# Expert outputs weighted when they leave PSUM and added to rows of y by indirect DMAs

## Chip, cores and metric

One core of a Trainium2 chip (trn2). The metric is the device time of one execution in microseconds (us), as the median of several runs.

## What is computed

One inference step of a two-layer decoder on 288 tokens (256 of a prompt and 8 sequences of 4): an attention layer with a dense feed-forward layer, then a state space layer (S5) with a mixture of experts. The change is in the mixture of experts, the last stage:

```python
logits = xn @ w_router + b_router
top_v, top_i = lax.top_k(logits, 2)                      # 2 of 8 experts for each token
gates = softmax(top_v)
combine = sum(one_hot(top_i, 8) * gates[..., None], 1)   # weight of each expert for each token
out = zeros((288, 1024))
for e in range(8):
    h = silu(xn @ w_gate[e]) * (xn @ w_up[e])            # 1024 -> 2816
    out = out + combine[:, e:e+1] * (h @ w_down[e])      # 2816 -> 1024
y = hp + out                                             # hp: the residual
```

## The kernel before

The kernel is written by hand, engine by engine: each of the five engines has its own instruction list, and semaphores tie them. Weights come in float32 and are split into a high and a low part, so that a product takes three matmuls (high times high, low times high, high times low).

**The loop over experts.** An expert's tokens, at most 128 (`CAP`), fill slots 0 to 127. The 2816 hidden columns of an expert are 22 chunks (`NF`) of 128, and one loop of `ck` runs over the 8 x 22 chunks on every engine, with `n, j = divmod(ck, 22)`: expert `n`, chunk `j`. For each chunk SP loads 1536 KB of weights into one of 8 slots, as soon as the chunk 8 before it is done. ACT casts the high parts (`gate_up_high`, L1323, two chunks ahead; `down_high`, L1328), and DVE subtracts to get the low parts (`gate_up_low`, L1956, two chunks ahead; `down_low`, L1963). PE multiplies (`gate_up`, 24 matmuls, L948 to L950), transposes the hidden block of the chunk before (`turn`, L958) and multiplies it with the down weights of two chunks before (`down`, L967 to L969), which add up in two PSUM banks over the expert. ACT and DVE form the hidden block in between (L1334, L1971) and split its transpose (L1340, L1979).

**The next expert's tokens** are prepared inside the loop, at places set by three numbers, `J_SELECT, J_FIND, J_GATHER = 2, 4, 12`. At `j == 2` DVE makes a one-hot matrix of tokens against slots (`select_first`, L1882). At `j == 4` PE multiplies it with the token numbers and norm factors (`find`, L921), and DVE copies the result out (`index`, L1891 and L1892); POOL then fetches those rows of x with an indirect DMA (`gather`, L2119). At `j == 12` to `19` PE transposes one 128-column piece of the eight at the end of each iteration (`turn_row`, L937), ACT writes its high part (`gathered_one`, L1313) and DVE its low part (`gathered_one`, L1949, which signals `xg_lo`). At `j == 0` of the next expert PE waits for all eight low parts:

```python
for ck in range(NE * NF + 2):                  # tensor, L974
    n, j = divmod(ck, NF)
    if ck < NE * NF:
        if j == 0:
            pe.wait_ge(S["xg_lo"], (n + 1) * KD)
        gate_up(chunk_at(ck), n % 2)
```

On ACT and DVE `gathered_one` stands at the end of the iteration, behind `gate_up_high`, `down_high` and `gate_up_low`.

**The output.** In the second iteration of the next expert ACT copies the finished sums to SBUF (`expert_sum`, L1345) and stores them to a scratch tensor, `yrow` (L1347). On DVE, in the seventh iteration of the first expert, `weights_of` works out the gates and, for each token, the two scratch rows that hold its expert outputs and their weights (`ranks`), in a chain of small operations that each wait for the one before. At the end POOL fetches those rows in six indirect DMAs (`rows_of`, L2132), DVE multiplies and adds them to the residual `res` (`add_rows`, L1933), and SP stores y in three DMAs (L452). Rounds for experts with more than 128 tokens exist behind a branch on all engines, which this input does not take.

**Before the first expert** POOL's first gather waits for the rows of x to be in DRAM (`xrow`, stored by SP, L433 and L434) and for `index(0, 0)`.

Of the kernel before, what the change touches and what calls it, by code (L numbers as in the profile page):

```python
# [65 lines left out]
J_SELECT, J_FIND, J_GATHER = 2, 4, 12  # L66
# [11 lines left out]
def layout(parts):  # L78
    at, n = {}, 0
    for name, size in parts:  # L80
# [7 lines left out]
                        ("rsel", 2), ("tok", 3)])  # L88
# [87 lines left out]
def build(nc, dr):  # L176
# [22 lines left out]
    slots_of = nc.alloc_sbuf_tensor("slots_of", [P, 2, 6], I32)  # L199
# [71 lines left out]
    tr, rsl = v(M_RT + 224, 3, 2), v(M_RT + 232, 2)  # L271
    plg, ssq, gsel = v(M_RT + 400, 3, KD, 8), v(M_RT + 592, 3, KD), v(M_RT + 616, 2, 6)
# [44 lines left out]
    def past_values(b, j, p):  # L317
# [9 lines left out]
        wt xt_mm xnat xr route pos_mm rexp cnt mS find_mm mIdx xin mg_mm mgu msil mh my yout dest yin0 yin1 yin2  # L327
        radd out dve act""".split()
# [48 lines left out]
    def _(sp):  # L377
# [56 lines left out]
        sp.dma_start(dr["xrow"][TP:T, :], res[0:NS, 2, :]).then_inc(S["xr"], 16)  # L434
        for ck in range(MSLOTS, NE * NF):
            sp.wait_ge(S["unit"], U_PRE + ck - MSLOTS + 1)
            expert_load(ck % MSLOTS, ck)
        sp.wait_ge(S["cnt"], 1)
        more = sp.value_load(counts[0:1, 0:1], min_val=0, max_val=T)
        with sp.If(more > CAP):  # L440
            sp.wait_ge(S["radd"], 6)
# [6 lines left out]
            sp.wait_ge(S["radd"], 12)  # L448
# [9 lines left out]
    def _(pe):  # L458
# [515 lines left out]
        for ck in range(NE * NF + 2):  # L974
# [35 lines left out]
    def _(act):  # L1010
# [280 lines left out]
        a(v(M_RT + 236, 1), eps, ACT.Sqrt)  # L1291
# [66 lines left out]
        for ck in range(NE * NF + 2):  # L1358
# [7 lines left out]
            if n and j == 1:  # L1366
                expert_sum(n - 1, dr["yrow"][(n - 1) * CAP:n * CAP])
# [6 lines left out]
        with act.If(more > CAP):  # L1374
            with act.Fori(0, (ROUNDS - 1) * NE) as m:
# [10 lines left out]
                expert_sum(m + NE, dr["ymore"][bass.ds(m * CAP, CAP)])  # L1386
# [3 lines left out]
    def _(dve):  # L1390
# [451 lines left out]
        link(V.tensor_copy(tr[:, :, 0], const("tok")))  # L1842
# [36 lines left out]
        def select(n, place, chosen):  # L1879

            for i, (t0, nt) in enumerate(BLK):
                m = V.tensor_scalar(onehot[0:nt, i, :], iota[0:nt, :], place(nt, i), chosen(nt, i), ALU.is_equal, ALU.mult)  # L1882
            m.then_inc(S["mS"], 1)

        def select_first(n):
            select(n, lambda nt, i: pos[0:nt, i, n:n + 1], lambda nt, i: selm[0:nt, i, n:n + 1])
# [8 lines left out]
        index(0, 0)  # L1895
# [4 lines left out]
        def weights_of():  # L1900
# [6 lines left out]
            for i in range(3):  # L1907
                m = V.tensor_tensor_scan(cum[:, i, :], ones[:, 0:8], selm[:, i, :], 0.0, ALU.mult, ALU.add)
            link(m)
            link(V.scalar_tensor_tensor(out=row, in0=iota[:, 0:8].unsqueeze(1).broadcast_to([P, 3, 8]), scalar=float(CAP),  # L1910
                                        in1=pos, op0=ALU.mult, op1=ALU.add))
            link(V.scalar_tensor_tensor(out=kept, in0=pos, scalar=float(CAP), in1=selm, op0=ALU.is_lt, op1=ALU.mult))
            ranks(0)

        cum, first, row, kept, prod = (v(M_RT + 400 + 24 * k, 3, 8) for k in range(5))

        def ranks(late):
            for r in range(2):
                link(V.scalar_tensor_tensor(out=first, in0=cum, scalar=float(r + 1), in1=kept, op0=ALU.is_equal, op1=ALU.mult))
                link(V.tensor_tensor(prod, first, comb, ALU.mult))  # L1920
                link(V.tensor_reduce(gsel[:, late].rearrange("p (i r) -> p i r", r=2)[:, :, r], prod, AX.X, ALU.add))
                link(V.tensor_tensor(prod, first, row, ALU.mult))
                link(V.tensor_reduce(v(M_RT + 530, 3), prod, AX.X, ALU.add))
                link(V.tensor_copy(slots_of[:, late].rearrange("p (i r) -> p i r", r=2)[:, :, r], v(M_RT + 530, 3)))
            dve.sem_inc(S["dest"], 1)

        def add_rows(late):
            for b in range(6):
                i, nt = b // 2, BLK[b // 2][1]
                dve.wait_ge(S[f"yin{b % 3}"], 16 * (b // 3 + 1 + 2 * late))  # L1930
                if b + late:
                    dve.wait_ge(S["radd"], 6 * late + b)
                V.scalar_tensor_tensor(out=res[0:nt, i, :], in0=ranked_rows(b)[0:nt, :], scalar=gsel[0:nt, late, b:b + 1],  # L1933
                                       in1=res[0:nt, i, :], op0=ALU.mult, op1=ALU.add).then_inc(S["radd"], 1)
# [50 lines left out]
        for ck in range(NE * NF + 2):  # L1985
# [8 lines left out]
            if n < NE - 1:  # L1994
                if j == J_SELECT:
                    select_first(n + 1)
                if j == J_FIND:
                    index(n + 1, (n + 1) % 2)
                if J_GATHER <= j < J_GATHER + KD:
                    gathered_one(n + 1, j - J_GATHER)  # L2000
            if ck == J_FIND + 2:
                weights_of()
        add_rows(0)
        more = dve.value_load(counts[0:1, 0:1], min_val=0, max_val=T)
        with dve.If(more > CAP):
# [6 lines left out]
            link(V.tensor_scalar(row, row, float(-CAP), None, ALU.add))
            for rd in range(2, ROUNDS):
                link(V.tensor_scalar(prod, pos, float(CAP * rd), float((NE - 1) * CAP), ALU.is_ge, ALU.mult))
                link(V.tensor_tensor(row, row, prod, ALU.add))
            link(V.scalar_tensor_tensor(out=kept, in0=pos, scalar=float(CAP), in1=selm, op0=ALU.is_ge, op1=ALU.mult))
            ranks(1)
            posc, selc = v(M_RT + 240, 24 * (ROUNDS - 1)), v(M_RT + 320, 24 * (ROUNDS - 1))
            with dve.Fori(0, (ROUNDS - 1) * NE) as m:
                column = lambda a: lambda nt, i: a[0:nt, bass.ds(m + 8 * (ROUNDS - 1) * i, 1)]  # L2020
                select(m + NE, column(posc), column(selc))
                index(m + NE, 0)
# [8 lines left out]
            add_rows(1)  # L2031
# [3 lines left out]
    def _(pool):  # L2035
# [85 lines left out]

        pool.wait_ge(S["xr"], 32)
        for n in range(NE):
            gather(n)

        def rows_of(late):
            pool.wait_ge(S["dest"], late + 1)
            for b in range(6):
                nt = BLK[b // 2][1]
                if b >= 3:  # L2130
                    pool.wait_ge(S[f"yin{b % 3}"], 16 * (1 + 2 * late))
                pool.indirect_dma_start(ranked_rows(b)[0:nt, :], None, dr["ymore" if late else "yrow"],  # L2132
                                        bass.IndirectOffsetOnAxis(ap=slots_of[0:nt, late, b:b + 1], axis=0)
                                        ).then_inc(S[f"yin{b % 3}"], 16)

        pool.wait_ge(S["yout"], 16 * NE)
        rows_of(0)
        pool.wait_ge(S["cnt"], 1)
        more = pool.value_load(counts[0:1, 0:1], min_val=0, max_val=T)
        with pool.If(more > CAP):  # L2140
            for n in range(NE, ROUNDS * NE):
                gather(n)
            pool.wait_ge(S["yout"], 16 * NE * ROUNDS)
            rows_of(1)
# [4 lines left out]
def shape_constants():  # L2149
# [24 lines left out]
    put("tok", np.stack([t0 + p for t0, _ in BLK], 1))  # L2174
# [94 lines left out]
OUTS = {"y": (T, D), "kout": (T, 256), "vout": (T, 256), "kiout": (T, 64), "s5p_out": (P, 2 * SJ),  # L2269
        "s5s_out": (2, P, SJ, NB)}  # L2270
SCRATCH = {"xrow": (T, D), "yrow": (NE * CAP, D), "ymore": ((ROUNDS - 1) * NE * CAP, D)}
# [24 lines left out]
```

## Time and profile before

| | us |
|---|---|
| median of 3 runs | 1647.05 (1642.23 to 1649.59) |
| the profiled execution, its own time | 1642.71 |
| its span, from the first to the last instruction | 1641.1 |
| PE busy in the span | 1447.5 (88%) |
| DVE busy | 1193.7 (73%) |
| ACT busy | 879.8 (54%) |
| POOL busy | 225.9 (14%) |
| mean granted TensorE clock | 0.914 |

Times in rows are in us from the span's start. The loop over experts runs from 829.11 (its first matmul) to about 1619.5, and the fetch, the additions and the store of y from there to the end. "Granted clock" is the share of TensorE's full speed that the chip allowed: 1.00 is 2.4 GHz, 0.50 is 1.2 GHz. A row of the timeline gives start, duration, engine, line, operation, tiles, and in brackets the engine's idle time before it with what ended that.

### The profile page before, as it was taken

The numbers are of one execution on the slowest core, as the hardware profiler recorded it, in microseconds if no ns is written. First come the engines' busy times: TensorE is split into PE (matmuls) and PEld (weight loads), VectorE is DVE, ScalarE is ACT, GpSimd is POOL, SyncE is SP. The second block draws the span as 40 slices with busy tenths as digits, with TensorE's granted clock in tenths as the row PEclk, the third lists the DMA queues.
The fourth block names the chain that finished last, engine by engine and source line by source line (L and its number), as shares of the span: only waits on it lengthen the run. The fifth ranks groups of instructions, "written<-read, shape, count | busy, mean of one in ns | idle before, by whom it ended". The sixth has DMA issues, their size and how long they took to land.

```text
span 1641.1 us, 27646 instructions
## 1 busy us (share of the span) xinstructions
PE 1447.5 (88%) x10403; PEld 1297.8 (79%) x10403; DVE 1193.7 (73%) x1859; ACT 879.8 (54%) x1580; POOL 225.9 (14%) x211
## 2 busy tenths in 40 slices
PE   6997978989998876359779999999999999999994
PEld 4784547879998775238678999999999999999993
DVE  3076553575453688994469999999999999999995
ACT  2322342424343321014467878778787777878872
POOL 3034000790000055360000000000000000000001
PEclk9998798999999955559889999999999999999997
DMA  9246624334445200005348999999999999999982
GB/s 349 80 142 183 219 93 158 116 116 154 155 170 192 88 2 1 1 1 200 144 149 342 355 375 358 375 362 361 377 350 375 356 372 364 354 380 353 373 325 101
DMA packets 52172, 382.35 MB, mean 233 GB/s; under 512 B 6658, under 2 KB 11842, under 8 KB 24002
## 3 DMA queue, kind: packets, MB, share of 16 engines
q1 hardware_dynamic: 46594, 366.71, 59.8%
q0 software_dynamic: 2848, 8.65, 1.6%
q10 hardware_dynamic: 2592, 5.15, 0.8%
q8 instruction: 86, 1.41, 0.3%
q14 instruction: 52, 0.43, 0.1%
HBM read 372.98 MB, written 7.51 MB: 232 GB/s over the span
## 4 chain that ended last, share of the span: by engine, by line
PE 78%; DVE 11%; issue 4%; ACT 3%; POOL 2%; DMA 2%; SPq 0%; ACTq 0%; DVEq 0%; POOLq 0%
PE ps L948 10%; PE ps L950 10%; PE ps L949 10%; PE ps L967 5%; PE ps L487 5%; PE ps L969 5%; PE ps L968 5%; PE ps L489 4%; PE ps L488 4%; PE ps L475 4%; POOL arena L2108 2%; DVE ring_lo L1424 2%; PE ps L805 2%; PE ps L807 1%; PE ps L806 1%
## 5 line engine op out<-in xcount | busy, mean ns | idle before, releaser
L948 PE MATMUL ps<-split 128*128 128x256 f32 x1408 | 405.0, 288 | 4.7 <-DVE split L1941 2.6
L950 PE MATMUL ps<-split 128*128 128x256 f32 x1408 | 399.6, 284 | 0.0
L1956 DVE TENSOR_TENSOR ring_lo<-ring,split 128x2048 fp32r<-128x2048 f32 x132 | 302.4, 2291 | 42.7 <-ACT split L1323 42.7
L949 PE MATMUL ps<-ring_lo,split 128*128 128x256 f32 x1056 | 299.7, 284 | 0.0
L948 PEld LDWEIGHTS ps<-split 128*128 128x128 f32 x1408 | 269.2, 191 | 15.4 <-DVE split L1941 3.0
L950 PEld LDWEIGHTS ps<-split 128*128 128x128 f32 x1408 | 269.1, 191 | 0.0
L1323 ACT CAST split<-ring 128x1024 fp32r<-128x1024 f32 x264 | 264.8, 1059 | 0.0
L1424 DVE TENSOR_TENSOR ring_lo<-ring,chunk_hi 128x1024 fp32r<-128x1024 f32 x100 | 144.3, 1445 | 164.4 <-ACT chunk_hi L1029 163.9
L1029 ACT CAST chunk_hi<-ring 128x1024 fp32r<-128x1024 f32 x100 | 104.7, 1048 | 210.6 <-PE ps L489 163.8
L949 PEld LDWEIGHTS ps<-ring_lo,split 128*128 128x128 f32 x1056 | 202.3, 192 | 3.2
L489 PE MATMUL ps<-xn_lo,chunk_hi 128*128 128x288 f32 x608 | 182.6, 300 | 0.0
L487 PE MATMUL ps<-xn_hi,chunk_hi 128*128 128x288 f32 x480 | 149.5, 311 | 24.9 <-DVE xn_lo L1406 12.1
L1963 DVE TENSOR_TENSOR ring_lo<-ring,split 128x1024 fp32r<-128x1024 f32 x132 | 160.3, 1214 | 0.0
L1334 ACT ACTIVATE arena<-ps,arena 128x128 f32<-128x128 f32 x176 | 64.7, 367 | 170.7 <-PE ps L950 170.7
L967 PE MATMUL ps<-split 128*128 128x512 f32 x352 | 153.3, 436 | 2.2 <-DVE more_lo L1963 2.2
L488 PE MATMUL ps<-xn_hi,ring_lo 128*128 128x288 f32 x480 | 145.2, 303 | 0.0
L1328 ACT CAST split<-ring 128x1024 fp32r<-128x1024 f32 x132 | 139.4, 1056 | 2.5 <-ACT arena L1345 2.0
L969 PE MATMUL ps<-split 128*128 128x512 f32 x352 | 138.4, 393 | 0.0
L2108 POOL TENSOR_TENSOR arena<-arena 128x512 f32<-128x512 f32 x64 | 83.0, 1298 | 288.1 <-DVE arena L1778 288.0
L487 PEld LDWEIGHTS ps<-xn_hi,chunk_hi 128*128 128x128 f32 x480 | 93.1, 194 | 33.0 <-issue 30.6
L489 PEld LDWEIGHTS ps<-xn_lo,chunk_hi 128*128 128x128 f32 x608 | 118.2, 194 | 0.0
L1956 DVE TENSOR_TENSOR more_lo<-arena,split 128x2048 fp32r<-128x2048 f32 x44 | 100.9, 2292 | 15.0 <-ACT split L1323 15.0
(333 smaller groups left out, 2824.6 us busy)
## 6 DMA issues: line engine op xcount, KB each, us to landing
ring<-wmoe SPq DMA_DIRECT2D x132, 1536.0 KB, 8.7
arena<-wmoe SPq DMA_DIRECT2D x44, 1536.0 KB, 8.9
ring<-wpre SPq DMA_DIRECT2D x41, 1536.0 KB, 6.7
ring<-ckv SPq DMA_DIRECT2D x32, 256.0 KB, 3.0
arena<-ckv SPq DMA_DIRECT2D x32, 256.0 KB, 2.9
yrow<-arena ACTq DMA_DIRECT2D x8, 512.0 KB, 10.2
arena<-cki SPq DMA_DIRECT2D x32, 64.0 KB, 2.0
arena<-cki POOLq DMA_DIRECT2D x32, 64.0 KB, 5.5
```

The source lines that it names most:

```text
L487: mm(out, chunk_hi[:, c % 2, w], hi[:, k, :], start=(k == 0), stop=False)
L488: mm(out, lo[:, w], hi[:, k, :], start=False, stop=False)
L489: m = mm(out, chunk_hi[:, c % 2, w], xn_lo_at[:, k, :], start=False, stop=(k == KD - 1))
L948: mm(o, xg_hi[:, buf, k, :], wg_hi[:, c.i % 2, w], start=(k == 0), stop=False)
L949: mm(o, xg_hi[:, buf, k, :], lo[:, w], start=False, stop=False)
L950: m = mm(o, xg_lo[:, buf, k, :], wg_hi[:, c.i % 2, w], start=False, stop=(k == KD - 1))
L967: mm(o, ht_hi[:, c.i % 2, :], wd_hi[:, c.i % 2, w], start=(j == 0), stop=False)
L969: m = mm(o, ht_lo[:, c.i % 2, :], wd_hi[:, c.i % 2, w], start=False, stop=(j == NF - 1))
L1323: cp(wg_hi[:, c.i % 2, w], moe_slot(slot)[:, w]).then_inc(S["mw_hi"], 1)
L1424: V.tensor_tensor(ring_lo[:, n % RING, w], ring[:, n % RING, w], chunk_hi[:, c % 2, :], ALU.subtract).then_inc(S["chunk_lo"], 1)
L1956: V.tensor_tensor(moe_slot_lo(slot)[:, w], moe_slot(slot)[:, w], wg_hi[:, c.i % 2, :], ALU.subtract).then_inc(S["mw_lo"], 1)
L1963: V.tensor_tensor(moe_slot_lo(slot)[:, w], moe_slot(slot)[:, w], wd_hi[:, c.i % 2, :], ALU.subtract).then_inc(S["wd_lo"], 1)
```

## The change

ACT multiplies the sums by the slot's gate when it copies them out of PSUM, and POOL adds the 128 rows to rows of y in DRAM with one indirect DMA with addition per expert. y first gets the residual (and 128 spare rows T to T+127, to which empty slots are added). The slot's gate is found with the same one-hot product as its token; for the first expert, whose gates come later, by a product of its own (`first_weight`). The scratch rows, `ranks`, the final fetch, additions and store go. The four places inside the loop move: `J_WEIGHT, J_SELECT, J_FIND, J_GATHER = 3, 6, 8, 14`, and `weights_of` moves from the seventh iteration to the second.

```diff
-J_SELECT, J_FIND, J_GATHER = 2, 4, 12
+J_WEIGHT, J_SELECT, J_FIND, J_GATHER = 3, 6, 8, 14
...
@@ SP, behind the two stores of xrow @@
+        sp.dma_start(dr["y"][0:TP, :].rearrange("(i p) c -> p i c", i=2), res[:, 0:2, :]).then_inc(S["out"], 16)
+        sp.dma_start(dr["y"][TP:T, :], res[0:NS, 2, :]).then_inc(S["out"], 16)
+        sp.dma_start(dr["y"][T:T + CAP, :], res[:, 0, :]).then_inc(S["out"], 16)
...
-        for i, (t0, nt) in enumerate(BLK):
-            sp.wait_ge(S["radd"], 2 * (i + 1))
-            sp.dma_start(dr["y"][t0:t0 + nt, :], res[0:nt, i, :]).then_inc(S["out"], 16)
+        sp.wait_ge(S["yout"], 16 * NE)
...
@@ PE @@
-                m = mm(ps[:, 7, 0:2], onehot[0:nt, i, :], tr[0:nt, i, :], start=(i == 0), stop=(i == 2))
+                m = mm(ps[:, 7, 0:3], onehot[0:nt, i, :], tr[0:nt, i, :], start=(i == 0), stop=(i == 2))
...
+        def first_weight():
+            pe.wait_ge(S["wgt"], 1)
+            for i, (t0, nt) in enumerate(BLK):
+                m = mm(ps[:, 7, 2:3], onehot[0:nt, i, :], tr[0:nt, i, 2:3], start=(i == 0), stop=(i == 2))
+            m.then_inc(S["wgt"], 1)
...
+            if ck == J_WEIGHT:
+                first_weight()
...
@@ ACT @@
-        def expert_sum(n, rows):
+        def expert_sum(n, buf):
             act.wait_ge(S["unit"], n * NF + (U_PRE + NF))
             act.wait_ge(S["yout"], n * 16)
-            cp(yn, ps[:, 3:5, :].rearrange("p a b -> p (a b)")).then_inc(S["my"], 1)
-            act.wait_ge(S["my"], n + 1)
-            act.dma_start(rows, yn).then_inc(S["yout"], 16)
+            a(yn, ps[:, 3:5, :].rearrange("p a b -> p (a b)"), ACT.Copy, scale=gsl[:, buf:buf + 1]).then_inc(S["my"], 1)
...
@@ DVE @@
-        def index(n, buf):
+        def index(n, buf, added):
 
             dve.wait_ge(S["find_mm"], n + 1)
-            V.tensor_copy(rsl[:, buf:buf + 1], ps[:, 7, 1:2])
+            dve.wait_ge(S["yout"], added * 16)
+            V.tensor_copy(gsl[:, buf:buf + 1], ps[:, 7, 2:3])
+            link(V.tensor_copy(rsl[:, buf:buf + 1], ps[:, 7, 1:2]))
+            link(V.scalar_tensor_tensor(out=far, in0=rsl[:, buf:buf + 1], scalar=0.0, in1=const("tok")[:, 3:4],
+                                        op0=ALU.is_equal, op1=ALU.mult))
+            V.tensor_tensor(slot_out[:, buf:buf + 1], far, ps[:, 7, 0:1], ALU.add)
             V.tensor_copy(slot_tok[:, :], ps[:, 7, 0:1]).then_inc(S["mIdx"], 1)
...
-            ranks(0)
...
+            V.tensor_copy(tr[:, :, 2], comb[:, :, 0]).then_inc(S["wgt"], 1)
...
                 if j == J_FIND:
-                    index(n + 1, (n + 1) % 2)
+                    index(n + 1, (n + 1) % 2, n)
...
-            if ck == J_FIND + 2:
+            if ck == 1:
                 weights_of()
-        add_rows(0)
+            if ck == J_WEIGHT:
+                dve.wait_ge(S["wgt"], 2)
+                V.tensor_copy(gsl[:, 0:1], ps[:, 7, 2:3])
...
@@ POOL @@
+        def add_rows(n):
+            buf = n % 2 if n < NE else 0
+            pool.wait_ge(S["my"], n + 1)
+            pool.indirect_dma_start(dr["y"], bass.IndirectOffsetOnAxis(ap=slot_out[:, buf:buf + 1], axis=0),
+                                    yn, None, compute_op=ALU.add).then_inc(S["yout"], 16)
+
         pool.wait_ge(S["xr"], 32)
+        gather(0)
+        pool.wait_ge(S["out"], 16 * 3)
         for n in range(NE):
-            gather(n)
...
-        pool.wait_ge(S["yout"], 16 * NE)
-        rows_of(0)
+            if n < NE - 1:
+                gather(n + 1)
+            add_rows(n)
```

Three places of the order of instructions matter; "waits" names the semaphores that an instruction waits for.

PE, before, around the last transposed piece for the second expert (L937, at the end of iteration 19 of the first; L967 to L969 are `down`, L948 to L950 `gate_up`):

```order
L967 MATMUL ps<-split 128x512
L968 MATMUL ps<-ring_lo,split 128x512
L969 MATMUL ps<-split 128x512
L937 MATMUL ps<-arena 128x128 [waits xg_lo]
L948 MATMUL ps<-split 128x256 [waits mh,mw_lo]
L949 MATMUL ps<-ring_lo,split 128x256
L950 MATMUL ps<-split 128x256
```

PE, now, the same piece (L938 now, at the end of iteration 21, the expert's last; lines are one further):

```order
L968 MATMUL ps<-split 128x512
L969 MATMUL ps<-ring_lo,split 128x512
L970 MATMUL ps<-split 128x512
L938 MATMUL ps<-arena 128x128 [waits xg_lo]
L949 MATMUL ps<-split 128x256 [waits mh,mw_lo,xg_lo]
L950 MATMUL ps<-more_lo,split 128x256
L951 MATMUL ps<-split 128x256
```

The piece moved by two chunks, and the instruction right behind it is now the first matmul of the next expert, which waits for `xg_lo`.

DVE, before, the chain of `weights_of` in the seventh iteration (behind `gate_up_low`, L1956), the first rows of its twenty instructions:

```order
L1956 TENSOR_TENSOR ring_lo<-ring,split 128x2048 [waits mw_hi]
L1903 TENSOR_TENSOR arena<-arena 128x24 [waits rexp]
L1904 TENSOR_REDUCE arena<-arena 128x3 [waits dve]
L1905 RECIPROCAL arena<-arena 128x3 [waits dve]
L1906 TENSOR_TENSOR arena<-arena 128x24 [waits dve]
L1908 SCALAR_TENSOR_TENSOR arena<-arena 128x8 [waits dve]
L1908 SCALAR_TENSOR_TENSOR arena<-arena 128x8 x2
L1910 SCALAR_TENSOR_TENSOR arena<-arena 128x24 [waits dve]
L1912 SCALAR_TENSOR_TENSOR arena<-arena 128x24 [waits dve]
L1919 SCALAR_TENSOR_TENSOR arena<-arena 128x24 [waits dve]
```

DVE, now, the whole chain, in the second iteration:

```order
L1938 TENSOR_TENSOR ring_lo<-ring,split 128x2048 [waits mw_hi]
L1912 TENSOR_TENSOR arena<-arena 128x24 [waits rexp]
L1913 TENSOR_REDUCE arena<-arena 128x3 [waits dve]
L1914 RECIPROCAL arena<-arena 128x3 [waits dve]
L1915 TENSOR_TENSOR arena<-arena 128x24 [waits dve]
L1916 COPY arena<-arena 128x3 [waits dve]
L1953 SCALAR_TENSOR_TENSOR arena<-ps,arena 128x128 [waits ht_mm,msil]
```

Five of the twenty instructions are left, five iterations earlier.

DVE, now, `index`, of which L1891 and L1892 were the whole before:

```order
L1896 COPY arena<-ps 128x1 [waits yout,find_mm]
L1897 COPY arena<-ps 128x1
L1898 SCALAR_TENSOR_TENSOR arena<-arena 128x1 [waits dve]
L1900 TENSOR_TENSOR slot_out<-arena,ps 128x1 [waits dve]
L1901 CAST slot_tok<-ps 128x1
```

Three instructions came in ahead of the one that releases POOL's gather (L1901), and the first now also waits for the expert before's rows to have been added (`yout`).

## Rows read from the trace of the kernel before

**Rows 1.** Chain of waits from the last matmul on: start, us, what

```profile
1619.57 1.02 ACT arena L1345
1620.61 2.62 DMA yrow<-arena
...
1623.49 4.51 DMA arena<-yrow,slots_of
...
1636.92 1.27 DVE arena L1933
```

**Rows 2.** DMA issues: y's smallest store; and L1347 (yrow), its times to landing

```profile
y<-arena SPq DMA_DIRECT2D x1, 128.0 KB, 2.2
...
DMA to landing us min/median/max: 2.6/10.2/10.9
```

**Rows 3.** Timeline around the eighth piece for the second expert

```profile
922.25 0.27 PE L937 MATMUL ps<-arena 128*128 128x128 f32 x1
922.28 0.36 PE L948 MATMUL ps<-split 128*128 128x256 f32 x1
...
924.21 0.38 ACT L1313 ACTIVATE split<-ps,arena 128x128 fp32r<-128x128 f32 x1
...
925.61 0.35 DVE L1949 SCALAR_TENSOR_TENSOR split<-ps,arena,split 128x128 fp32r<-128x128 f32 x1
```

**Rows 4.** Timeline of PE, earlier stages: restarts after waits of PE

```profile
244.59 0.58 PE L487 MATMUL ps<-xn_hi,chunk_hi 128*128 128x288 f32 x1 [3.65 <-DVE xn_lo L1406]
...
289.57 0.37 PE L487 MATMUL ps<-xn_hi,chunk_hi 128*128 128x288 f32 x1 [4.25 <-DVE xn_lo L1406]
...
342.47 0.58 PE L487 MATMUL ps<-xn_hi,chunk_hi 128*128 128x288 f32 x1 [2.62 <-DVE ring_lo L1424]
...
542.20 0.37 PE L487 MATMUL ps<-xn_hi,chunk_hi 128*128 128x288 f32 x1 [4.18 <-DVE xn_lo L1406]
```

**Rows 5.** Stretches behind them, PE alone: us, busy (matmuls), granted clock, DMA share, GB/s

```profile
244.60:249.60 5.00, 5.00 (x21) 0.50 0.99 414
...
290.70:294.00 3.30, 3.30 (x13) 0.50 0.00 0
...
342.50:348.60 6.10, 6.07 (x24) 0.50 0.00 0
...
543.30:546.60 3.30, 3.30 (x14) 0.50 0.00 0
546.70:550.00 3.30, 3.30 (x25) 1.00 0.00 0
```

**Rows 6.** Timeline of PE: `turn` (L958), one per chunk, in the first expert

```profile
846.10 0.27 PE L958 MATMUL ps<-arena 128*128 128x128 f32 x1
...
850.47 0.27 PE L958 MATMUL ps<-arena 128*128 128x128 f32 x1
...
855.69 0.27 PE L958 MATMUL ps<-arena 128*128 128x128 f32 x1
...
864.44 0.27 PE L958 MATMUL ps<-arena 128*128 128x128 f32 x1
...
876.25 0.27 PE L958 MATMUL ps<-arena 128*128 128x128 f32 x1
```

**Rows 7.** Timeline of DVE: the chain of `weights_of` begins

```profile
864.92 0.18 DVE L1903 TENSOR_TENSOR arena<-arena 128x24 f32<-128x24 f32 x1
865.14 0.18 DVE L1904 TENSOR_REDUCE arena<-arena 128x3 f32<-128x24 f32 x1
```

**Rows 8.** Chain of waits ahead of the first expert

```profile
807.95 4.92 DMA xrow<-arena
...
816.62 7.90 DMA arena<-xrow,slot_tok
```

**Rows 9.** Timeline: `expert_sum` on ACT, and `index` on DVE, in the second expert

```profile
940.87 1.02 ACT L1345 COPY arena<-ps 128x1024 f32<-128x1024 f32 x1
...
956.33 0.15 DVE L1891 COPY arena<-ps 128x1 f32<-128x1 f32 x1
```

More of the change, by code:

```diff
@@ L270, in build @@
     wt, junk = v(S_WT, KD, 136), v(S_JUNK, 2, 3, 128)
-    tr, rsl = v(M_RT + 224, 3, 2), v(M_RT + 232, 2)
-    plg, ssq, gsel = v(M_RT + 400, 3, KD, 8), v(M_RT + 592, 3, KD), v(M_RT + 616, 2, 6)
+    tr, rsl, gsl, far = v(M_RT + 224, 3, 3), v(M_RT + 234, 2), v(M_RT + 237, 2), v(M_RT + 236, 1)
+    plg, ssq = v(M_RT + 400, 3, KD, 8), v(M_RT + 592, 3, KD)
     sil, he = v(M_SI, 2, CAP), v(M_H, 2, CAP)
@@ L326, in build @@
         ht_mm ht_hi ht_lo bu_mm pin gin gs po_out y_mm zin z last carry xs hs ys_mm zs_in zs gl_mm gsg glu
-        wt xt_mm xnat xr route pos_mm rexp cnt mS find_mm mIdx xin mg_mm mgu msil mh my yout dest yin0 yin1 yin2
-        radd out dve act""".split()
+        wt xt_mm xnat xr route pos_mm rexp cnt mS find_mm mIdx xin mg_mm mgu msil mh my yout wgt out dve act""".split()
     S = {n: nc.alloc_semaphore(n) for n in names}
@@ L1290, in _ @@
                 natural(mch - 1)
-        a(v(M_RT + 236, 1), eps, ACT.Sqrt)
+        a(v(M_RT + 239, 1), eps, ACT.Sqrt)
         natural(7)
@@ L1366, in _ @@
             if n and j == 1:
-                expert_sum(n - 1, dr["yrow"][(n - 1) * CAP:n * CAP])
+                expert_sum(n - 1, (n - 1) % 2)
             if ck < NE * NF:
@@ L1877, in _, with select @@
         link(V.tensor_copy(pos[0:NS, 2, :], ps[0:NS, 6, 16:24]))
-        def select(n, place, chosen):
+        def select(n, place, chosen, weight):
             for i, (t0, nt) in enumerate(BLK):
                 m = V.tensor_scalar(onehot[0:nt, i, :], iota[0:nt, :], place(nt, i), chosen(nt, i), ALU.is_equal, ALU.mult)
+                if weight:
+                    m = V.tensor_copy(tr[0:nt, i, 2:3], weight(nt, i))
             m.then_inc(S["mS"], 1)
         def select_first(n):
-            select(n, lambda nt, i: pos[0:nt, i, n:n + 1], lambda nt, i: selm[0:nt, i, n:n + 1])
-        def index(n, buf):
+            select(n, lambda nt, i: pos[0:nt, i, n:n + 1], lambda nt, i: selm[0:nt, i, n:n + 1],
+                   (lambda nt, i: comb[0:nt, i, n:n + 1]) if n else None)
+        def index(n, buf, added):
             dve.wait_ge(S["find_mm"], n + 1)
-            V.tensor_copy(rsl[:, buf:buf + 1], ps[:, 7, 1:2])
+            dve.wait_ge(S["yout"], added * 16)
[4 more added lines that the diff above has]
+            V.tensor_tensor(slot_out[:, buf:buf + 1], far, ps[:, 7, 0:1], ALU.add)
             V.tensor_copy(slot_tok[:, :], ps[:, 7, 0:1]).then_inc(S["mIdx"], 1)
         select_first(0)
-        index(0, 0)
+        index(0, 0, 0)
         dve.wait_ge(S["pos_mm"], 2)
@@ L1906, in weights_of @@
             link(V.tensor_tensor(comb, comb, v(M_RT + 208, 3).unsqueeze(2).broadcast_to([P, 3, 8]), ALU.mult))
[L1907 to L1912, printed above, removed]
-            ranks(0)
[L1915 to L1934, printed above, removed]
+            V.tensor_copy(tr[:, :, 2], comb[:, :, 0]).then_inc(S["wgt"], 1)
         def gathered_all(n, buf):
@@ L2010, in _ @@
                 m = V.tensor_copy(selr[:, :, w], selm)
+                V.tensor_copy(wgtr[:, :, w], comb)
             link(m)
[L2012 to L2018, printed above, removed]
+            posc, selc, wgtc = (v(M_RT + o, 24 * (ROUNDS - 1)) for o in (240, 320, 400))
             with dve.Fori(0, (ROUNDS - 1) * NE) as m:
                 column = lambda a: lambda nt, i: a[0:nt, bass.ds(m + 8 * (ROUNDS - 1) * i, 1)]
-                select(m + NE, column(posc), column(selc))
-                index(m + NE, 0)
+                select(m + NE, column(posc), column(selc), column(wgtc))
+                index(m + NE, 0, m + NE)
                 gathered_all(m + NE, 0)
@@ L2142, in _ @@
                 gather(n)
-            pool.wait_ge(S["yout"], 16 * NE * ROUNDS)
-            rows_of(1)
+                add_rows(n)
     block.__exit__(None, None, None)
@@ L2173, in shape_constants @@
     put("rsel", (p[:, None] // 16) % 2 == np.arange(2)[None, :])
-    put("tok", np.stack([t0 + p for t0, _ in BLK], 1))
+    put("tok", np.stack([t0 + p for t0, _ in BLK] + [T + p], 1))
     cb = np.zeros((P, NCONSTB), np.float32)
@@ L2266, in lay_out @@
     return {k: np.ascontiguousarray(a) for k, a in out.items()}
-OUTS = {"y": (T, D), "kout": (T, 256), "vout": (T, 256), "kiout": (T, 64), "s5p_out": (P, 2 * SJ),
+OUTS = {"y": (T + CAP, D), "kout": (T, 256), "vout": (T, 256), "kiout": (T, 64), "s5p_out": (P, 2 * SJ),
         "s5s_out": (2, P, SJ, NB)}
-SCRATCH = {"xrow": (T, D), "yrow": (NE * CAP, D), "ymore": ((ROUNDS - 1) * NE * CAP, D)}
+SCRATCH = {"xrow": (T, D)}
 def kernel(**inputs):
```

27 lines of the change are left out of this document (7 added, 20 removed).

## Prediction

> **What bounds the kernel now.** I read the page first: PE is busy for 88% of the span, and the other engines for less. Then the chain of waits. Inside the loop over experts it stays on PE's matmuls. Behind the last matmul it goes ACT, store, fetch, addition, store: the copy L1345 ends at 1620.6 [rows 1], and the span at 1641.1, so 20.5 us are left there for the change to shorten. Third, the timeline of the loop, to see how close each engine comes to making PE wait. One chunk takes PE 4.37 us (850.47 less 846.10, rows of `turn`) [rows 6], and the loop has 176 of them. Work that the change takes from ACT, DVE or the DMA queues inside the loop is therefore worth nothing unless PE waits for it, and work that it moves can cost if PE then has to wait.
>
> **The end: 13.2 us less.** What goes: the store of yrow (2.62), the fetches (the first takes 4.51), the additions and the store of y, in all the 20.5 us above. What takes their place: POOL is released, issues the addition, SP sees it land. A release took 0.26 (yrow landed at 1623.23, the fetch was issued at 1623.49) [rows 1]; I take it twice. An addition in DRAM is in no row. It moves 128 rows of 4 KB, as the fetch of 4.51 does, and on top of it a write follows the read; the nearest row for one more trip to DRAM is y's smallest store, 2.2 [rows 2]. Sum 6.7, so 7.2 to 7.3 us in place of 20.5: a gain of 13.2. Bounds: a plain store of the same 512 KB landed in 2.6 at best and in 10.9 at worst, amid weight loads [rows 2], which makes the gain 17.4 or 9.1. I take the middle because nothing else uses the DMA engines then, but the read must come before the write.
>
> A sentence from a page beside it: the Trainium skill, DMA: Bandwidth & Descriptors, section on the anatomy of a DMA on the SWDGE (gpsimd) path, gives such a DMA about 2.0 us and its bytes over 436 GB/s; as an estimate that is 3.2 us here, and the sum would come out 3.5 us lower by it. The trace disagrees already for the fetch, with 4.51 us for the same bytes.
>
> **The change of expert: 26.2 us more.** The eighth piece of the next expert's tokens moved from iteration 19 to 21, the expert's last, so PE's next instruction is the matmul that waits for its low part. How long that low part takes is in the trace, since iteration 19 had the same neighbours: PE began the transpose at 922.25 and went on with the next chunk at 922.28; ACT wrote the high part only at 924.21, and DVE the low part from 925.61 to 925.96 [rows 3]. They are that late because `gathered_one` stands behind the splits of the weights two chunks ahead, which nobody needs at that moment; the late piece cannot overtake them. In iteration 19 it cost nothing: PE had other chunks of the same expert. Now PE starts at about 926.02 (0.06 for the semaphore, an estimate) instead of 922.28: 3.74 us, at 7 changes of expert, 26.2 us. Behind PE's waiting matmul stands everything PE does, and then ACT's and DVE's `gate` of that chunk. PE does not catch up: it is the bound before and after.
>
> **The clock behind each such wait: 13.6 us more.** Four times in earlier stages PE waited 2.62 to 4.25 us and then went on with dense matmuls [rows 4]. Each time the granted clock was at 0.50 (1.2 GHz) afterwards, for 5.0, 3.3, 6.1 and 3.3 us [rows 5], 4.4 on average. What half the clock costs: 14 matmuls in 3.30 us against 25 in the next 3.30 us [rows 5], so 44% of the time is lost, 1.95 us a wait, 13.6 for seven. Bounds: 0 if the clock holds, and 7 x 6.1 x 0.44 = 18.8. I take the average of the four, because a wait of 3.74 lies between theirs.
>
> A page on the same: the Trainium skill, TensorE: Matmul & The Clock Gate, section Terms, puts the penalty at the throttled time times one minus the granted share, so half of it; by that seven stretches of 4.4 us cost 15.4, 1.8 us more than by the row.
>
> **The gates: 2.2 us less.** PE's `turn` came at 864.44 and then, two chunks later, at 876.25: 11.81 instead of 8.74, 3.07 us lost while DVE did the twenty operations of `weights_of` in that iteration [rows 6]. Now five are left (four of them each waiting for the one before, at 0.22 a step [rows 7]), about 1.1 us in the second iteration, where DVE's split for the next chunk was done about 1 us before PE wanted it (estimated from the timeline of DVE; the cover, if gone, costs a few tenths). Against that, `first_weight` is a second `find`: the `turn` behind the first `find` came 5.22 us after the one before it, 0.85 more than 4.37 [rows 6]. Net -2.2. The seven other `find`s only move.
>
> **Ahead of the first expert: 0.6 us more.** `index(0, 0)` has three more operations before it releases POOL's gather, two of them with a wait: 2 x 0.22 and two overlapped ones of less than 0.1. That gather (7.90 us) is on the path [rows 8]. SP's three new stores of y, 1664 KB, queue behind the stores of xrow, which landed at 812.87, nearly 4 us before the gather was issued at 816.62 [rows 8]; at the 230 KB per us of those stores (1152 KB in 4.92) they would end about 820 and meet only the first half of the gather. I cost them at 0, at most 3.
>
> **At no cost:** ACT's scaling (the same copy with a factor, and less waiting than with the store behind it); three more copies of a column in `select`; the bytes of the additions, one read of 512 KB more per expert than the stores of yrow had.
>
> **Sum.** -13.2 + 26.2 + 13.6 - 2.2 + 0.6 = +25.0. The profiled execution took 1642.71, so 1667.7; it lies 4.3 below the median of the three runs shown and near their lowest, and from that median the sum is 1672.0. I forecast 1670, 1.4% slower. A measurement of this kernel can tell about 0.5%, 8.2 us, from no change.
>
> **Rivals.**
> - *The wait comes, the clock holds.* Then +11.4: 1654.1 to 1658.4. Against it stand four waits out of four in rows 4 and 5; for it, that those stages had sparser work ahead of some waits. 12%.
> - *Late additions.* The addition takes far longer than any store here. Up to 20 us it costs at the end alone: the sum ends at 1675 to 1684. Beyond that DVE comes in: `index` now waits in iteration 8 for the addition that POOL issues in iteration 1. In time of the trace before that is from 942.15 (copy at 940.87, 1.02, release 0.26) to 956.33 plus four chunks, 973.8: 31.7 us [rows 9]; each us beyond it would hold up DVE and the next gather in seven experts. A store amid the loads took at most 10.9 [rows 2]. 12%.
> - *No wait at the change of expert: faster.* If ACT and DVE wrote the last piece before the weights' splits, or ran further ahead, PE would find it ready. Then the gains stand alone: -13.2 - 2.2 + 0.6 = -14.8, 1628 to 1632. It decides at a wait of 2.1 us (14.8 over 7, with the clock held): below that the kernel gets faster. The rows give 3.74, and the order of both engines' instructions is fixed. 4%.
>
> **How the numbers follow.** The forecast case has 70%, and 2% are left for what I haven't thought of. Inside it the addition gives 4 us either way, the clock +5 or -3 (each wait 3.3 or 6.1 us of half clock, mixed), the base 2: 1660 to 1680. With most of the first rival and the short part of the second the range is 1656 to 1682. Slower by over 0.5% (above 1655.3): the forecast case, the late additions and most of the first rival, 0.89; within 0.5%: 0.07; faster: 0.04.
>
> **What would show it.** Right: PE idle for about 3.5 us seven times, some 100 us apart, ended by DVE's `gathered_one`, with granted clock 0.50 behind; the chain's end from ACT's copy to the last instruction about 7 us long; no gap in PE near the seventh chunk. Wrong: matmuls of the next expert going on directly behind the eighth transpose, a landing time of the additions above 11 us, or DVE's `index` waiting for a DMA.

## Result, and the profile after

| | before | after |
|---|---|---|
| median of four runs, us | 1645.28 (1642.23 to 1649.59) | 1668.30 (1667.97 to 1669.41) |
| the profiled execution, its own time | 1642.71 | 1668.50 |
| its span | 1641.1 | 1666.8 |
| PE busy | 1447.5 (88%) | 1457.1 (87%) |
| POOL busy | 225.9 (14%) | 238.7 (14%) |
| mean granted clock | 0.914 | 0.911 |

The ratio is 1.0139, 95% interval 1.0113 to 1.0165: slower by 1.4%, 1668.30 against the 1670 forecast. Between the medians that is 23.0 us, between the two profiled executions 25.8.

**The change of expert.** The list of PE's waits (engine, tile and line, what it waited for; total us, times, longest), from 840 us to the last matmul:

```profile
PE ps L949 <- DVE split L1931: 24.4, 7, 3.5
PE ps L968 <- DVE more_lo L1945: 1.1, 2, 0.7
```

L949 is the first matmul of `gate_up`, L1931 DVE's `gathered_one`. PE has hardly another wait in the loop. One of the seven in the timeline of PE (L959 is `turn`, L938 `turn_row`):

```profile
1030.26 0.27 PE L959 MATMUL ps<-arena 128*128 128x128 f32 x1
...
1031.76 0.27 PE L938 MATMUL ps<-arena 128*128 128x128 f32 x1
1035.51 0.39 PE L949 MATMUL ps<-split 128*128 128x256 f32 x1 [3.48 <-DVE split L1931]
...
1039.98 0.28 PE L959 MATMUL ps<-arena 128*128 128x128 f32 x1
...
1044.36 0.27 PE L959 MATMUL ps<-arena 128*128 128x128 f32 x1
```

From the turned row to the next matmul 3.75 us pass, where PE used to go on at once [rows 3]. From one `turn` to the next it is 9.72 in place of the 4.48 of an iteration with a turned row. Over the seven changes these intervals are 9.40, 9.72, 9.68, 10.54, 9.71, 9.72 and 10.55; less 7 x 4.48 that is 38.0 us more, and the intervals behind them add 1.0: **39.0 us** in all, of which 7 x 3.75 = 26.3 are the wait. Windows of PE behind that wait (us, busy and matmuls, granted clock, DMA share, GB/s) hold most of the rest:

```profile
1035.50:1038.90 3.40, 3.39 (x18) 0.60 0.75 300
1038.90:1042.30 3.40, 3.40 (x22) 0.89 0.07 28
```

PE is busy throughout, at a granted clock of 0.60 and then 0.89 on average. Behind the fourth and the seventh wait, the two with the long intervals, the clock stayed at half for longer (the fourth, which ended at 1241.82):

```profile
1241.90:1247.80 5.90, 5.90 (x27) 0.50 0.46 178
```

In all, half clock took 6.0 us behind each of these two and 3.3 to 3.4 us behind each of the other five. Why the row is late, in ACT's and DVE's timeline:

```profile
1030.87 2.00 ACT L1326 CAST split<-ring 128x1024 fp32r<-128x1024 f32 x2
1032.76 1.05 ACT L1331 CAST split<-ring 128x1024 fp32r<-128x1024 f32 x1
1033.71 0.38 ACT L1316 ACTIVATE split<-ps,arena 128x128 fp32r<-128x128 f32 x1
...
1032.90 2.29 DVE L1938 TENSOR_TENSOR ring_lo<-ring,split 128x2048 fp32r<-128x2048 f32 x1 [0.33 <-ACT split L1326]
1035.11 0.34 DVE L1931 SCALAR_TENSOR_TENSOR split<-ps,arena,split 128x128 fp32r<-128x128 f32 x1
```

The row is in PSUM at 1032.03. ACT copies it (L1316) only behind three casts for chunks that nobody waits for yet, and DVE splits it (L1931) behind a 2.29 us subtraction.

**The end.** ACT's scaled copy and POOL's last addition in the timeline, and the times to landing of the eight additions:

```profile
1656.06 1.11 ACT L1348 ACTIVATE arena<-ps,arena 128x1024 f32<-128x1024 f32 x1 [3.27 <-PE ps L970]
...
1657.46 1.55 POOL L2103 DMA_INDIRECT y<-arena,slot_out  x1 [88.63 <-ACT arena L1348]
```

```profile
DMA to landing us min/median/max: 7.1/13.4/14.2
```

From the copy's end, 1657.17, to the span's end are 9.6 us, where 20.5 stood before [rows 1]. 7.1 is the last addition, alone on the DMA engines; the median of all eight, seven of them amid weight loads, is 13.4. From 1657.46 + 7.1 = 1664.6 another 2.2 us pass. The list of waits of SP's queue puts 2.0 of these to PE's sequencer, where before it put 0.4:

```profile
SPq L2120 <- PEq L2120: 2.0, 1, 2.0
```

```profile
SPq L2146 <- PEq L2146: 0.4, 1, 0.4
```

PE is named because its signal comes last. Each engine's list closes with a `DRAIN` on that line, and the last instructions of all engines wait for one another; POOL's `DRAIN` is the long one (durations in ns, start in us):

```profile
L2120 POOLq DRAIN  x1: 8607/8607/8607, 1658.0 to 1658.0; - x1
L2120 PEldq DRAIN  x1: 73/73/73, 1659.3 to 1659.3; - x1
```

It ends at 1666.6, 2.0 us behind the landing of the addition that POOL itself issued, and the span ends 0.2 us later. In the kernel before, POOL's closing `DRAIN` began at 1631.9 and took 5.96 us; it was over at 1637.9, while DVE was still adding.

**The first expert.** Timeline of PE:

```profile
835.05 0.27 PE L959 MATMUL ps<-arena 128*128 128x128 f32 x1
...
837.09 0.39 PE L949 MATMUL ps<-split 128*128 128x256 f32 x1 [1.76 <-DVE ring_lo L1938]
...
841.47 0.36 PE L959 MATMUL ps<-arena 128*128 128x128 f32 x1
...
845.93 0.27 PE L959 MATMUL ps<-arena 128*128 128x128 f32 x1
...
851.15 0.27 PE L959 MATMUL ps<-arena 128*128 128x128 f32 x1
855.52 0.27 PE L959 MATMUL ps<-arena 128*128 128x128 f32 x1
859.88 0.27 PE L959 MATMUL ps<-arena 128*128 128x128 f32 x1
864.25 0.27 PE L959 MATMUL ps<-arena 128*128 128x128 f32 x1
868.62 0.27 PE L959 MATMUL ps<-arena 128*128 128x128 f32 x1
```

The gap of 3.07 us in iterations 6 and 7 [rows 6] is gone; `first_weight` costs 5.22 - 4.37 = 0.85. The first interval, though, is 6.42 us, and 4.92 before. The wait of 1.76 us in it is followed by half clock:

```profile
838.30:841.60 3.30, 3.30 (x19) 0.50 0.00 0
```

**The account** is made from the first `turn` to the end of the span, since the stage ahead of it, of almost the same code, varied by some 7 us from profile to profile. Before: 1641.1 - 836.81 = 804.3. After: 1666.8 - 835.05 = 831.8, 27.5 more. The terms: changes of expert +39.0; the end from the last matmul on -10.8 (21.6 to 10.8); gap in the first expert -3.07; `first_weight` +0.85; the first two intervals +1.6. Sum +27.6. Where the end has to be left out, the loop alone is counted, from the first `turn` to the last (the line of `turn`, before and after, with first and last start):

```profile
L958 PE MATMUL ps<-arena x176: 269/271/330, 836.8 to 1614.9; 128*128 128x128 f32 x176
L959 PE MATMUL ps<-arena x176: 270/271/415, 835.0 to 1651.4; 128*128 128x128 f32 x176
```

That is 778.1 before and 816.3 after.

### The profile page after: what moved, and what is told of

It reads as the page before. It is cut to its first block, busy times and chain, and to the rows that moved or that the text cites. A ratio compares the mean times of both kernels' runs of the same rounds, so it can differ in the third digit from the quotient of the medians.

```text
span 1666.8 us, 27675 instructions
## 1 busy us (share of the span) xinstructions
PE 1457.1 (87%) x10409; PEld 1307.1 (78%) x10409; DVE 1194.0 (72%) x1883; ACT 880.5 (53%) x1580; POOL 238.7 (14%) x213
## 4 chain that ended last, share of the span: by engine, by line
PE 71%; DVE 12%; issue 9%; ACT 4%; POOL 2%; DMA 1%; SPq 0%; DVEq 0%; POOLq 0%; ACTq 0%
PE ps L949 9%; PE ps L951 9%; PE ps L950 9%; PE ps L482 4%; PE ps L968 4%; PE ps L970 4%; PE ps L969 4%; PE ps L483 4%; PE ps L484 4%; PE ps L470 3%; DVE ring_lo L1425 2%; POOL arena L2086 2%; PE ps L800 2%; PE ps L802 1%; PE ps L801 1%
## 5 line engine op out<-in xcount | busy, mean ns | idle before, releaser
L949 PE MATMUL ps<-split 128*128 128x256 f32 x1408 | 411.0, 292 | 28.7 <-DVE split L1931 24.4
L951 PE MATMUL ps<-split 128*128 128x256 f32 x1408 | 405.4, 288 | 0.0
L949 PEld LDWEIGHTS ps<-split 128*128 128x128 f32 x1408 | 275.3, 196 | 41.0 <-DVE split L1931 26.9
L950 PE MATMUL ps<-ring_lo,split 128*128 128x256 f32 x1056 | 304.3, 288 | 0.0
L951 PEld LDWEIGHTS ps<-split 128*128 128x128 f32 x1408 | 275.3, 196 | 0.0
L1425 DVE TENSOR_TENSOR ring_lo<-ring,chunk_hi 128x1024 fp32r<-128x1024 f32 x100 | 149.6, 1498 | 159.6 <-ACT chunk_hi L1032 159.1
L950 PEld LDWEIGHTS ps<-ring_lo,split 128*128 128x128 f32 x1056 | 207.1, 196 | 3.3
L1938 DVE TENSOR_TENSOR more_lo<-arena,split 128x2048 fp32r<-128x2048 f32 x44 | 100.8, 2291 | 14.4 <-ACT split L1326 14.2
```

The costliest lines, as they stand in the source:

```text
L949: mm(o, xg_hi[:, buf, k, :], wg_hi[:, c.i % 2, w], start=(k == 0), stop=False)
L950: mm(o, xg_hi[:, buf, k, :], lo[:, w], start=False, stop=False)
L951: m = mm(o, xg_lo[:, buf, k, :], wg_hi[:, c.i % 2, w], start=False, stop=(k == KD - 1))
L1425: V.tensor_tensor(ring_lo[:, n % RING, w], ring[:, n % RING, w], chunk_hi[:, c % 2, :], ALU.subtract).then_inc(S["chunk_lo"], 1)
L1938: V.tensor_tensor(moe_slot_lo(slot)[:, w], moe_slot(slot)[:, w], wg_hi[:, c.i % 2, :], ALU.subtract).then_inc(S["mw_lo"], 1)
```

## Experiments

"Loop and end" is the time from the first `turn` to the end of the span in the profile of each; it is 804.3 before and 831.8 after. "Measured" gives the median in us, then its ratio to the kernel before with the 95% interval. Medians and ratios are against runs of the kernel before on the same chip (medians 1643.54 for the first four, 1642.06 for the next three, 1645.23 for the last).

**1. The rows two iterations earlier**

```diff
-J_WEIGHT, J_SELECT, J_FIND, J_GATHER = 3, 6, 8, 14
+J_WEIGHT, J_SELECT, J_FIND, J_GATHER = 3, 4, 6, 12
```

> The changed kernel with J_SELECT, J_FIND, J_GATHER = 4, 6, 12 in place of 6, 8, 14: the eight turned rows of the next expert stand two iterations earlier, all three steps as far apart as they were. Theory (the place of the last turned row costs 39.0 us in all: seven waits of 3.48 us at the change of expert and the half clock behind them): the seven waits are gone, the seven intervals around the change of expert fall from 9.4 to 10.55 us back to 4.37 to 4.48, and the time is 1668.3 - 39 = about 1629, below the kernel before. Rival (the additions on POOL's queue and the work that each expert gained on ACT and DVE slow the loop, the wait only shows it): the loop stays as long, 1660 to 1670.

Measured: 1633.32, ratio 0.9923 (0.9895 to 0.9951); loop and end 792.5, 39.3 less than after; the loop alone 777.4, **39.0 less**. The waits on `gathered_one` are gone; from 850 us on the list of PE's waits has one line left:

```profile
PE ps L968 <- DVE more_lo L1945: 1.1, 2, 0.7
```

The median came out 4 us above the 1629 expected; its runs lie from 1629.08 to 1637.52, and the profiled one reached its first `turn` 6.2 us later than the one after. The loop alone is 0.7 us shorter than before, as the three terms of the first expert give it (-3.07 + 0.85 + 1.6). So the additions, still there, cost the loop nothing to be seen: the rival falls.

**2. One iteration earlier**

```diff
-J_WEIGHT, J_SELECT, J_FIND, J_GATHER = 3, 6, 8, 14
+J_WEIGHT, J_SELECT, J_FIND, J_GATHER = 3, 5, 7, 13
```

> The changed kernel with J_SELECT, J_FIND, J_GATHER = 5, 7, 13: one iteration earlier. The last turned row is issued one iteration of 4.37 us before the change of expert, and its high and low parts are ready 3.75 us behind it. Theory (a wait stands only where the two parts are later than PE's next use): 3.75 is under 4.37, no wait, about 1629, the same as with two iterations. Rival (the rows share ACT's and DVE's queues with the chunk, and one iteration is not enough because they are taken behind the chunk's own steps): a part of the wait stays and pulls the clock down too, 1635 to 1655.

Measured: 1631.58, ratio 0.9922 (0.9896 to 0.9949); loop and end 792.9. No wait. The last row in the timeline of PE and of DVE:

```profile
1029.02 0.27 PE L938 MATMUL ps<-arena 128*128 128x128 f32 x1
...
1032.39 0.34 DVE L1931 SCALAR_TENSOR_TENSOR split<-ps,arena,split 128x128 fp32r<-128x128 f32 x1
```

The row is as late as ever, 3.71 us from its turn to its low part, and one iteration of other work hides that. One place in the table of four decides between 1.4% slower and 0.8% faster.

**3. The late place alone, in the kernel before**

```diff
-J_SELECT, J_FIND, J_GATHER = 2, 4, 12
+J_SELECT, J_FIND, J_GATHER = 2, 4, 14
```

> The kernel before with J_GATHER = 14 in place of 12 and nothing else. Theory: the seven waits of 3.5 us and the half clock behind them appear here too, without any addition to y: 1645.3 + 39 = about 1684 (1680 to 1688). Rival (the waits come from the additions or the scaled copy): no change, 1643 to 1648.

Measured: 1683.46, ratio 1.0241 (1.0208 to 1.0274); loop and end 844.8, 40.5 more than before; the loop alone 817.2, 39.1 more (the rest is in the end). PE's waits show the same total as the changed kernel:

```profile
PE ps L948 <- DVE split L1949: 24.4, 7, 3.5
```

The wait needs no addition and no scaled copy. It alone costs the loop what it cost the changed kernel, 39 us.

**4. PE kept at work during the wait**

```diff
+                if j == NF - 1:
+                    pe.wait_ge(S["mw_lo"], chunk_at(ck + 1).q + 1)
+                    pe.wait_ge(S["mh"], chunk_at(ck + 1).q - 2)
+                    for f in range(28):
+                        w = slice((f % KD) * 256, (f % KD + 1) * 256)
+                        mm(ps[:, (ck + 1) % 3, 0:256], xg_hi[:, n % 2, f % KD, :], wg_hi[:, (ck + 1) % 2, w],
+                           start=True, stop=True)
```

> The changed kernel with 28 matmuls of 128x256 that nothing reads, between the last turned row and the next expert's first matmul, so that PE works for some 3.1 of the 3.48 us of each of the seven waits; what the program waits for stays as it was. Theory (of the 39.0 us about 26 are the wait itself and 12.9 the half clock behind it): the granted clock stays at 1.00 behind the change of expert and the time is 1668.3 - 12.9 = about 1655.4 (1653 to 1658). Rival (the intervals behind the wait are long because the engines have to fall into step again): 1666 to 1670, and slower if the fillers last beyond the wait.

Measured: 1656.38, ratio 1.0081 (1.0050 to 1.0112); loop and end 818.2, 13.6 less than after; the loop alone 803.8, 12.6 less. The other 1.0 is the end, where the last addition landed in 6.2 us instead of 7.1. Timeline of PE and windows at one change of expert:

```profile
1035.94 0.27 PE L959 MATMUL ps<-arena 128*128 128x128 f32 x1
...
1037.44 0.27 PE L938 MATMUL ps<-arena 128*128 128x128 f32 x1
1037.47 3.59 PE L1000 MATMUL ps<-split 128*128 128x256 f32 x28
1041.21 0.39 PE L949 MATMUL ps<-split 128*128 128x256 f32 x1 [0.15 <-DVE split L1938]
...
1044.19 0.27 PE L959 MATMUL ps<-arena 128*128 128x128 f32 x1
```

```profile
1037.40:1041.10 3.70, 3.66 (x30) 1.00 0.95 349
1041.20:1044.60 3.40, 3.39 (x27) 1.00 0.73 298
```

The next expert's first matmul still starts 3.77 us behind the turned row, but the granted clock is 1.00 behind it, and 27 matmuls go through where 18 did. The interval is 8.25: 3.77 over 4.48, so all that is left is the wait. The engines need no time to fall into step. Matmuls that nobody reads gave back a third of the loss.

**5. A scatter without addition**

```diff
-                                    yn, None, compute_op=ALU.add).then_inc(S["yout"], 16)
+                                    yn, None).then_inc(S["yout"], 16)
```

on the kernel of experiment 2.

> The kernel with J_GATHER = 13 and the indirect DMA without its addition: rows of y are overwritten, so the sum over the experts is left out. Theory (the addition at the end is long because each row of y is read before it is written): the last transfer's 7.1 us from issue to landing falls to the 2 to 5 us of a store or a fetch of such rows, POOL's 1.55 us of issue falls towards the 0.96 of a gather, and the end behind the last matmul shrinks by 2 to 5 us. Rival (the price is that of an indirect write to memory, with or without addition): 6.2 to 7.2 us, no change of the end.

Measured: 1628.01, ratio 0.9911 (0.9881 to 0.9940); loop and end 789.6, 3.3 less than with the addition. The line of that DMA on POOL (durations, ns) and its times to landing:

```profile
L2103 POOL DMA_INDIRECT y<-arena,slot_out x8: 976/1882/1884, 940.5 to 1619.1; - x8
...
DMA to landing us min/median/max: 4.0/10.7/11.2
```

With addition the same kernel shows 1547/2482/2512 ns and 7.2/13.3/14.0 us. So the addition costs POOL some 0.6 us per DMA and 3.2 us in landing at the end (one profile without it, 4.0; 2.2 to 3.3 by the six kernels with it, whose last addition landed in 6.2 to 7.3). That the 3.2 us are the read ahead of the write fits, but wasn't taken apart further.

**6. The last row first in the queues** (ACT shown; on DVE the same, between `turned_low` and `down_low`)

```diff
                 turned_high(chunk_at(ck - 1))
+            if n < NE - 1 and j == NF - 1:
+                gathered_one(n + 1, KD - 1)
             if ck + 2 < NE * NF:
                 gate_up_high(chunk_at(ck + 2), loaded(ck + 2))
...
-                if n < NE - 1 and J_GATHER <= j < J_GATHER + KD:
+                if n < NE - 1 and J_GATHER <= j < NF - 1:
                     gathered_one(n + 1, j - J_GATHER)
```

> The changed kernel, J_GATHER still 14, but in iteration 21 ACT copies the turned row ahead of chunk ck + 2's 3.05 us of casts, and DVE splits it ahead of its 1.22 and 2.29 us, in place of behind them. Theory (3.48 us is not the row's own latency but its place in the two queues): ACT's copy stands at about 0.3 us behind the row, DVE's behind that, and each of the seven waits falls to 0.8 to 1.3 us; the casts begin some 1.2 us later, of which DVE's 0.35 us of slack and ACT's 0.85 hide a part, so a wait of up to 1 us may follow. Without half clock behind it 1668.3 - 39 + 7 x (1.1 to 2.1) = 1637 to 1644; with a half clock at each as it was, 1650 to 1657. Rival (the turn, the copy and the split themselves take 3.5 us): 1666 to 1670.

Measured: 1637.75, ratio 0.9971 (0.9954 to 0.9987); loop and end 800.4, 31.4 less than after; the loop alone 785.2. Timeline of PE, then ACT and DVE, at one change of expert:

```profile
1029.27 0.27 PE L938 MATMUL ps<-arena 128*128 128x128 f32 x1
1030.38 0.39 PE L949 MATMUL ps<-split 128*128 128x256 f32 x1 [0.84 <-DVE split L1933]
...
1029.58 0.37 ACT L1316 ACTIVATE split<-ps,arena 128x128 fp32r<-128x128 f32 x1 [1.08 <-PE ps L938]
1029.85 1.99 ACT L1326 CAST split<-ring 128x1024 fp32r<-128x1024 f32 x2
...
1029.98 0.35 DVE L1933 SCALAR_TENSOR_TENSOR split<-ps,arena,split 128x128 fp32r<-128x128 f32 x1 [1.02 <-ACT split L1316]
```

The turn, the copy and the split themselves take 1.11 us; the other 2.64 of the 3.75 were queue. The casts now start some 1.45 us later on ACT (1.08 us waiting for the row, 0.37 copying it), and no later wait came of it: 7 x 1.11 = 7.8, which is what the loop alone is longer than in experiment 2 (777.4). Behind these waits of 0.84 us the granted clock stayed at 1.00.

**7. The chain of the ranks spread out, in the kernel before**

```diff
-            if ck == J_FIND + 2:
-                weights_of()
+            if ck in (6, 7, 8, 9, 10, 20, 21, 22, 23, 25):
+                for step in weights[0:2]:
+                    step()
+                weights = weights[2:]
```

where `weights` holds the steps of `weights_of` and `ranks(0)` in their order.

> The kernel before with the same steps of the weights and the ranks, but two at a time over iterations 6 to 10 and 20 to 22, in place of all in iteration 6. Theory (that chain on DVE makes gates 6 and 7 late and costs 3.07 us): the intervals 5.31 and 6.50 us fall to 4.37 to 4.6, the first expert is 2 to 3 us shorter, and the time is 1640 to 1641.5, by itself hardly to be told from 1643.5. Rival (the gap comes from the end of the first loads and not from the chain): the two intervals stay.

Measured: 1639.67, ratio 0.9993 (0.9971 to 1.0014), which by itself tells nothing. The timeline of `turn` does:

```profile
864.26 0.27 PE L958 MATMUL ps<-arena 128*128 128x128 f32 x1
...
868.63 0.27 PE L958 MATMUL ps<-arena 128*128 128x128 f32 x1
...
873.00 0.27 PE L958 MATMUL ps<-arena 128*128 128x128 f32 x1
```

8.74 for two chunks, where it was 11.81 [rows 6], and the first expert, from turn to turn, 98.5 us in place of 101.5. The chain was the cause.

**8. A shorter index ahead of the first expert**

```diff
+            if isinstance(n, int) and n == 0:
+                V.tensor_copy(rsl[:, buf:buf + 1], ps[:, 7, 1:2])
+                V.tensor_copy(slot_tok[:, :], ps[:, 7, 0:1]).then_inc(S["mIdx"], 1)
+                return
...
+            if ck == 4:
+                link(V.scalar_tensor_tensor(out=far, in0=rsl[:, 0:1], scalar=0.0, in1=const("tok")[:, 3:4],
+                                            op0=ALU.is_equal, op1=ALU.mult))
+                V.tensor_tensor(slot_out[:, 0:1], far, ps[:, 7, 0:1], ALU.add)
```

on the kernel of experiment 2.

> The kernel with J_GATHER = 13, where the index of the first expert does only what it did in the kernel before (two copies, the second the token), and the row of y and the test for an empty slot are worked out in iteration 4. Theory (the added steps ahead of the first expert move PE's 1.76 us wait against what it did before it, and the clock falls behind that wait): the first interval between turns falls from 6.4 to 4.9 us, the gather starts 0.45 us earlier, and the time is 1629 to 1630. Rival (the fall belongs to the wait itself or to something else of the change): the interval stays at 6.4 us and only the 0.45 us are gained, 1631.

Measured: 1631.18, ratio 0.9903 (0.9865 to 0.9940); loop and end 793.0. PE waited 9.05 us for the gather in place of 9.44, so the index is worth its 0.4 us (9.44 to 9.62 in the six kernels with the longer one). The first interval stayed at 6.21, and PE's wait at 1.76: my theory on the first interval falls.

## Why the prediction was right

- **The end, -13.2 forecast: -10.8.** Right in kind, inside its bounds (17.4 to 9.1), 2.4 short. The addition landed in 7.1 where the sum had 6.7. That these are so close is in part luck: by experiment 5 the transfer without the addition takes 4.0 and the addition puts 3.2 on top, where the sum had 4.51 and 2.2. What was mis-sized is the last step, the release of SP, costed at 0.26: 2.2 us pass. They are POOL's: in all ten profiles its closing `DRAIN` ended 1.9 to 2.0 us behind the landing of its own last indirect DMA, with the addition and without (experiment 5), and that was hidden as long as other work stood at the end. The sum had no term for it, so 9.6 us stand behind the copy where about 7 was named. The Trainium skill (DMA: Bandwidth & Descriptors, the section on the anatomy of a DMA on the SWDGE path) gives 2.0 us plus the bytes over 436 GB/s, an estimate of 3.2 us: near the plain scatter's 4.0, less than half of the addition's 7.1.
- **The change of expert, +26.2: 26.3.** Seven times 3.75, for the reason given: the row stands behind casts that nobody needs at that moment. Experiments 2, 3 and 6 show it from three sides.
- **The clock, +13.6: 12.7** (39.0 less 26.3). Experiment 4 takes it away and the loop alone gives back 12.6. Half clock lasted 4.1 us on average where the sum had 4.4, 28.9 us in all, and 12.7 of 28.9 is 44%, the price that the sum took from [rows 5]. The first rival, that the clock holds, would have been 1654 to 1658; that is what experiment 4 measured with the clock held by force. The Trainium skill (TensorE: Matmul & The Clock Gate, section Terms) sets the loss at the throttled time times the share not granted. In the two windows shown that is 3.40 x 0.40 + 3.40 x 0.11 = 1.73 us, against 9.72 - 4.48 - 3.75 = 1.49 by the intervals at that change: a little high, as before. The case against the first rival was weaker than "four waits out of four": the kernel before has another wait of that size, 2.94 us, with dense matmuls and full clock behind it (timeline, then window, of PE):

```profile
138.59 0.62 PE L616 MATMUL ps<-arena 64*32 64x256 f32 x2 [2.94 <-DVEq L1542]
```

```profile
138.60:142.00 3.40, 3.40 (x14) 1.00 0.01 2
```

Behind the seven waits of 3.5 us in the kernel after, and the seven in experiment 3, half clock came every time.

- **The gates, -2.2: -2.2** (-3.07 and +0.85), shown by experiment 7 and the timeline. The chain that was spread there has twenty-one instructions, not twenty.
- **Ahead of the first expert, +0.6:** `index(0, 0)` takes 0.67 us in place of 0.22 up to the token; PE's wait for the gather was 9.54 us after and 9.03 before, 0.51 more, so y's stores added next to nothing.
- **Not in the sum:** 1.6 us in the first two intervals, about what 3.4 us of half clock cost at that price. With it, and the end 2.4 short, less 0.9 for the clock, the terms from the first `turn` on (24.4) were 3.2 us low; the profiled execution then reached its first `turn` 1.8 us earlier than the one before, and its 25.8 fell next to the 25.0 partly by luck. The forecast of 1670 stood between this sum on the profiled execution and on the median.
- **Late additions** cost nothing, though one sign named for being wrong did show: amid weight loads the additions landed in 13.4 us (median) and up to 14.2, above the 11 named and the 10.9 of the slowest store of yrow [rows 2]. Nothing waited for them: POOL issued the second expert's at 1048.28, and `index` reads at 1079.82. Only the last one, alone on the DMA engines, is on the path.
- **No wait, 1628 to 1632:** wrong for this change, and right as a number: that is experiment 2's 1631.58, the version that beats both kernels.

## What to carry to other kernels

When a step moves towards the place that needs it, count what stands ahead of it in every in-order queue it passes through, not its own duration: here 1.1 us of work took 3.75. A loop that one engine bounds paid such waits in full here, and again in the clock behind them: 26 and 13 us, more than the 11 saved at the end. (The waits of 0.84 us in experiment 6 did not pay the second price.) A kernel that ends with an indirect DMA of POOL's paid another 2.0 us behind its landing here. Before judging such a change, try its neighbours in the table: one iteration made the difference between 23 us lost and 12 gained.

## What was not expected

- The addition amid weight loads took 13.4 us to land and POOL 2.48 us to issue, against 7.1 and 1.55 alone. A plain scatter showed 10.7 and 1.88 against 4.0 and 0.98. Nothing waited for it here.
- In the first expert PE's wait for the weights' low part was 1.76 or 1.77 us in all seven kernels with the change, and the granted clock fell behind it (0.67 for 3.4 us in the profile after, 0.66 to 0.71 in the others); in the three without, it was 1.68 or 1.69, and the clock stayed at 1.00. What adds 0.08 us, and whether the clock falls for that or for what PE did earlier, stays open.
- The stage ahead of the experts ended anywhere from 835.05 to 842.20 us in ten profiles, with PE's waits of nearly the same length (164 to 169 us in sum); between 100 and 200 us the granted clock was 0.85 in the profile after and 0.78 in that of experiment 2. Differences of a few us between single executions are read from a common point of the timeline, not from the totals.
